# Taking all filler matmuls out of a two-block transformer kernel on one core

## The reference, cut to what matters

```
h   = rmsnorm(x, g)               # sum of squares over 1024 features, per token
f   = (silu(h @ w_gate) * (h @ w_up)) @ w_down
x   = x + scale * rmsnorm(f, g')  # in the second block f is normed too
```

## Time and profile before

| | |
|---|---|
| median of 3 runs | 1871.64 us (1868.79 to 1875.58) |
| span of the profiled execution | 1873.7 us |
| TensorE matmul busy | 1795.8 us, 96% of the span |
| TensorE weight load busy | 1748.1 us, 93% |
| VectorE busy | 1253.9 us, 67% |
| ScalarE busy | 879.5 us, 47% |
| mean granted TensorE clock | 0.983 of full speed |

### The profile page before, as it was taken

One profiled execution on the slowest core, in us unless ns is written; L12 is line 12 of the kernel. 1 busy time (PEld: TensorE's weight loads), 2 busy tenths in 40 slices (PEclk: granted clock), 3 DMA queues, 4 the chain that ended last, 5 costly groups with the idle time before them and its releaser, 6 DMA issues.

```text
span 1873.7 us, 34817 instructions
## 1 busy us (share of the span) xinstructions
PE 1795.8 (96%) x14318; PEld 1748.1 (93%) x14318; DVE 1253.9 (67%) x1567; ACT 879.5 (47%) x1093; POOL 187.0 (10%) x198
## 2 busy tenths in 40 slices
PE   6987999999999999999999999989999998999987
PEld 4977999998999999999978999989999996999986
DVE  7889877777674456555876755566555686765555
ACT  4573434345543344334576533345433477543333
POOL 2023211110200011000130000011000111100001
PEclk9998999999999999999999999999999999999998
DMA  9775798856455544454322355433554340454540
GB/s 365 269 271 210 270 330 314 296 209 245 158 203 179 182 155 175 174 190 179 118 109 105 143 180 180 178 132 116 202 179 179 114 179 24 146 198 175 195 140 23
DMA packets 60369, 346.14 MB, mean 185 GB/s; under 512 B 6362, under 2 KB 10602, under 8 KB 26224
## 3 DMA queue, kind: packets, MB, share of 16 engines
q1 hardware_dynamic: 40640, 281.24, 41.2%
q0 software_dynamic: 16512, 59.84, 8.9%
q10 hardware_dynamic: 3120, 3.67, 0.6%
HBM read 341.59 MB, written 3.15 MB: 184 GB/s over the span
## 4 chain that ended last, share of the span: by engine, by line
PE 86%; DVE 6%; ACT 3%; DMA 2%; issue 2%; POOL 1%; POOLq 0%; SPq 0%; ACTq 0%; DVEq 0%
PE bank L488 25%; PE bank L490 25%; PE bank L489 25%; PE bank L562 3%; PE bank L556 2%; PE bank L640 1%; DMA work<-bias_rows 1%; ACT w_hi L946 1%; DVE w_lo L1352 1%; PE bank L661 1%; DMA raw<-in_stream 1%; POOL sq L424 1%; PE bank L650 1%; PE bank L519 1%; PE bank L517 1%
## 5 line engine op out<-in xcount | busy, mean ns | idle before, releaser
L488 PE MATMUL bank<-a_hi,w_hi 128*128 128x256 f32 x3048 | 869.4, 285 | 14.1 <-DVE a_lo L1677 8.4
L489 PE MATMUL bank<-a_lo,w_hi 128*128 128x256 f32 x3048 | 864.7, 284 | 0.0
L490 PE MATMUL bank<-a_hi,w_lo 128*128 128x256 f32 x3048 | 864.7, 284 | 0.0
L488 PEld LDWEIGHTS bank<-a_hi,w_hi 128*128 128x128 f32 x3048 | 587.3, 193 | 16.8 <-issue 10.7
L489 PEld LDWEIGHTS bank<-a_lo,w_hi 128*128 128x128 f32 x3048 | 587.3, 193 | 0.3
L490 PEld LDWEIGHTS bank<-a_hi,w_lo 128*128 128x128 f32 x3048 | 587.1, 193 | 0.0
L1526 DVE TENSOR_TENSOR w_lo<-raw,w_hi 128x2048 fp32r<-128x2048 f32 x144 | 330.0, 2292 | 271.0 <-ACT w_hi L1024 270.9
L1024 ACT CAST w_hi<-raw 128x2048 fp32r<-128x2048 f32 x144 | 273.4, 1899 | 283.3 <-PE bank L490 283.3
L1352 DVE TENSOR_TENSOR w_lo<-raw,w_hi 128x2048 fp32r<-128x2048 f32 x119 | 273.3, 2301 | 121.9 <-ACT w_hi L946 121.7
L488 PE MATMUL bank<-hid_hi,w_hi 128*128 128x256 f32 x1096 | 310.8, 284 | 0.4 <-DVE hid_lo L1521 0.4
L489 PE MATMUL bank<-hid_lo,w_hi 128*128 128x256 f32 x1096 | 310.2, 283 | 0.0
(11 more groups left out here) (207 smaller groups left out, 1590.9 us busy)
## 6 DMA issues: line engine op xcount, KB each, us to landing
raw<-in_stream SPq DMA_DIRECT2D x266, 1024.0 KB, 4.8
shared<-in_mods POOLq DMA_DIRECT2D x102, 512.0 KB, 6.5
work<-in_mods POOLq DMA_DIRECT2D x8, 512.0 KB, 9.5
bias_rows<-work ACTq DMA_DIRECT2D x1, 2048.0 KB, 21.6
x<-in_x_t SPq DMA_DIRECT2D x1, 1024.0 KB, 5.9
work<-bias_rows ACTq DMA_DIRECT2D x1, 1024.0 KB, 20.8
out_t<-x SPq DMA_DIRECT2D x8, 128.0 KB, 1.8
sq<-in_mods POOLq DMA_DIRECT2D x1, 512.0 KB, 7.0
```

Of the source, the lines that this page charges most:

```text
L488: pe.matmul(out, w_h, v_h, start=start, stop=False, skip_group_check=True)
L489: pe.matmul(out, w_h, v_l, start=False, stop=False, skip_group_check=True)
L490: return pe.matmul(out, w_l, v_h, start=False, stop=stop, skip_group_check=True)
```

## The change

`keep_warm` and `norm_between` are removed with all their calls. Where `norm_between` stood, `norm_stat` stands alone. Nothing else changes: the order, the waits and the other engines' programs are as before.

```diff
-            def keep_warm(n, b=1):
-                for _ in range(n):
-                    pe.matmul(bank[b][:, 0:P], ones[:, :], ident[:, :], start=True, stop=True)
-            def norm_between(n, first=WARM_BEFORE, then=WARM_AFTER):
-                keep_warm(first)
-                norm_stat(n)
-                keep_warm(then)
...
-            keep_warm(8)
             mod_reduce(G_MIX0, 7)
             need_slab(B_WIN)
-            keep_warm(9)
             need_slab(B_WIN + 1)
...
-            keep_warm(14, 5)
             for hd in range(LHEADS):
...
-            keep_warm(16)
             mod_reduce(G_A0, 2)
-            keep_warm(12)
...
-            keep_warm(8)
             norm_stat(N_FFN0)
             mod_reduce(G_B0, 3)
-            keep_warm(8)
             ffn(0, B_FFN0, A_FFN0)
             mod_reduce(G_KV, 1)
-            keep_warm(6, 2)
             norm_stat(N_KV)
...
-            norm_between(N_FFN1, 2)
+            norm_stat(N_FFN1)
             ffn(1, B_FFN1, A_FFN1)
-            norm_between(N_FIN, 14)
+            norm_stat(N_FIN)
...
-                norm_between(norm2(l, L_POST1))
+                norm_stat(norm2(l, L_POST1))
...
-                norm_between(norm2(l, L_POSTMIX))
+                norm_stat(norm2(l, L_POSTMIX))
...
-                norm_between(norm2(l, L_POST2), WARM_BEFORE, 0)
+                norm_stat(norm2(l, L_POST2))
...
-                norm_between(norm2(l, L_POSTPLE), WARM_BEFORE + 6, WARM_AFTER if l + 1 < LAYERS2 else 0)
+                norm_stat(norm2(l, L_POSTPLE))
...
-WARM_BEFORE, WARM_AFTER = 10, 24
```

## The result

Over all its runs the changed kernel takes 1886.4 us (median of 20), the kernel before 1875.9 (median of 20); the ratio is 1.0056, with a 95% interval of 1.0043 to 1.0069, so 8 to 13 us more. The forecast was 1879, or +7.4 us on a median of 1871.6, inside its range of 1870 to 1887; as a ratio it was 1.0040, just under the interval. The median of before was 4 us lower when the forecast was made, because it came from three runs only; that is 4.2 of the 7.4 us by which 1886.4 lies above 1879, and the range held the time with 0.6 us to spare.

A forecast was written before the change was run, and what follows sets the result against it. TensorE was taken to bound the kernel. Losses 14.0 + 1.2 + 1.2 + 1.4 + 0.4 = 18.2 us, less 10.8 saved, make 7.4 slower: 1871.6 + 7.4 = 1879 us, range 1870 to 1887 (8 in 10).

The forecast's parts named there:

- What bounds the kernel: Whole kernel: TensorE, busy for 96% of the span; a microsecond it gains or loses between dense stretches is one of the span.
- VectorE's fifth chunk: Behind norm_stat at L_POST1: the fifth chunk of a_lo is only 0.2 us early, hides no loss, would cap a gain.
- What the removal gives back: Around norm_stat: fillers still running when the next real instruction could start (overrun) cost 10.8 us, which is saved.
- the terms ahead and behind: Overrun ahead of norm_stat at six places, 4.8 us, and behind it at seven places, 6.0 us.
- The price of a gap: Idle gap ahead of dense matmuls lowers the clock and costs 1.5 to 2.0 us, 1.75 taken; eight places, 14.0 us.
- The eight dense runs behind new gaps: Matmuls of the gates and those behind norm_stat at seven places: slowed by 14.0 us in all (12.0 to 16.0).
- the factor of the prediction: Share of TensorE's working time at half clock that is lost, from matmul starts: 0.44, as in 4.55 x 0.44 = 2.0 us.
- The small terms: norm_stat slower at N_FIN 1.2 us, L_POSTPLE 1.4; gap behind mod_reduce at N_FFN0 1.2; first 42 us and G_A0 0.4.
- Two terms were set to zero: norm_stat at L_POST2 (twice) and at N_FFN0: already at low clock before the change, so 0 us.
- The clock isn't lost: Rival: real work around the gaps keeps the clock up and the overrun is saved, 1861 us; chance 0.08.
- Loss and gain cancel: Rival: each of eight gaps costs 1.3 us and the uncertain items stay at their lower ends, 1873 us; chance 0.25.
- Two stretches behind each gap: Rival: clock stays low for 6.8 us filled with matmuls behind each gap, 3.0 us a place, 1889 us; chance 0.12.

The follow-up runs named there:

- The trimmed kernel: Kernel before with fillers only cut back to what fits each place's gap (52 of 357 matmuls out): ratio 0.9939, 1862.2 us.
- the kernel with filled gaps: The trimmed kernel with fillers added in the long idle stretches that the fillers of before left: ratio to the kernel before 0.9904, 1857.2 us.

## Why the prediction was right, step by step

**What bounds the kernel** was right: TensorE. Where it lost time, the end moved by as much, but for VectorE's fifth chunk.

**What the removal gives back**, 10.8 us: right in sum, as far as the runs can tell, and near at each place. At the six places with overrun ahead the gaps got shorter by 1.34, 1.50, 0.96, 1.46, 1.10 and 1.48 us, 7.8 in all, where the terms ahead and behind make 8.4. The trimmed kernel gained 11.8 us (1862.2 against 1874.0; 7.7 to 15.4 by its interval). The fifth chunk, of which the prediction said that it would cap a gain, did.

**The price of a gap**, 1.75 us: right in kind, short in size. The eight dense runs behind new gaps lost 2.5, 2.1, 1.4, 1.5, 2.6, 1.7, 1.9 and 2.7 us, 16.4 us instead of 14.0, a mean of 2.05. The range of 1.5 to 2.0 was read from two stretches of the earlier trace rows; the mean lies just above it because many of the new low stretches are double ones of which the gap fills only a small part (5.8 of 6.7 us were worked behind L_POSTMIX). By the half-clock rule of the Trainium skill (page "TensorE: Matmul & The Clock Gate", section "HAM oscillation — how this bites in real kernels", a penalty of half the throttled time), those 5.83 us would cost 2.9, an estimate. The starts gave 2.6, which is 0.44 of them, the factor of the prediction.

**The small terms.** norm_stat at N_FIN took twice its time, as thought (3.57 us with its tail, behind 3.33 us of idleness). Two terms were set to zero that aren't. At L_POST2 the prediction saw that norm_stat was at half clock already, and stopped there. With the idleness 2.2 us longer the low clock outlasts norm_stat: the 240 product matmuls behind it lost 1.1 us in each layer. In the changed kernel's timeline of TensorE the first two start 0.57 us apart, against 0.36 in the kernel before:

```profile
1241.02 3.78 PE L556 MATMUL bank<-sq,ones 128*128 128x256 f32 x8 [7.68 <-POOL sq L424]
1244.24 0.78 PE L488 MATMUL bank<-hid_hi,w_hi 128*128 128x256 f32 x1
1244.81 0.41 PE L489 MATMUL bank<-hid_lo,w_hi 128*128 128x256 f32 x1
```

And at N_FFN0, where 1.2 us were taken, this trace has 3.7: norm_stat waits behind 6.12 us instead of 2.29, mod_reduce is at half clock for a part, and then comes the dense loss of 1.5 us. With only that place changed it was 1.7, of which the dense loss was again 1.5; the rest of the 3.7 lies within what the gap does with its fillers in place.

**The rivals.** "The clock isn't lost" is out: the low clock lay in or right behind every gap of 4 us and more between two matmuls. "Loss and gain cancel" is out by the time, 8 to 13 us, and by its price of 1.3 us a gap. "Two stretches behind each gap" holds for some places. The prediction called itself wrong if low stretches reached 6 us into dense work, and at three of the eight places they nearly or just did: 5.7 us at the gates, 5.9 and 6.05 behind the two L_POSTMIX, for 2.5 to 2.7 us each where this rival had 3.0. At the other five it was 3.2 to 4.9 us.

**Luck, and what stays open.** From one trace of each, the places with fillers sum to 14.8 us without the start and attention, where the same terms of the forecast make 7.1, and the timed difference is 8 to 13. Of the 7.7 us between, 2.4 are the price of a gap, 2.2 L_POST2 and 2.5 N_FFN0. So the mechanism and its signs were right, the losses came out low, and it is partly luck that the sum still came near the timed difference. The stretches of low clock and the late transfers fell differently in each trace, so two traces can't give the mean; that the rest of the difference is this, is argued and not shown.

## What to carry to other kernels

Filler matmuls are neither good nor bad: judge each group by its gap. Compare the end of the last filler with the end of the operand that the next real instruction needs; what runs over is lost, but for what the next wait would have taken anyway (0.4 to 0.6 us at five places here). An idle time of 3.7 to 4.8 us cost 1.4 to 2.7 us of half-speed work behind it at every place here, one of 3.1 us cost it in some traces and not in others, and one of about 2 us at two places of seven. Here fillers fitted to the gaps gained 0.96%, while taking all out lost 0.56%: a saving of 11 us (an estimate from the gaps) and a loss about twice as large hid in one small number.

## What the runs showed of the hardware that was not expected

- Gaps of equal length (4.50 us of idleness at four places) cost 1.5 to 2.7 us from one place to the next in the same trace, in good part by whether one or two low stretches follow. Gaps of about 2 us lowered the clock at two of seven places, gaps of 3.7 to 4.8 us at all; a gap of 3.1 us at one and the same place lowered it in the trace of before and left it alone in three experiments. The Trainium skill's advice to leave no long idle gap between bursts (page "TensorE: Matmul & The Clock Gate", section "Why this matters for your kernels") agrees with these runs.
- The clock falls inside attention too, where TensorE is busy with idle times of at most 1.8 us between: 0 to 2.9 us in each of the two long stages and trace, with equal code. It may be a part of the spread of the runs of before (1869 to 1883 us), as may the late transfer in the short stage. The trimmed kernel's five runs lay within 2.2 us (1860.9 to 1863.0), the six of the kernel with filled gaps within 3.1; these are fewer runs than the 20 of before.
- Fillers at half clock take twice as long too, and then run over gaps that they fitted into: at N_FIN, 6.71 us instead of 5.52.
